# Turning attention probabilities one step later, in 20 steps instead of 19

## The reference: what is computed

```
s = q k^T * scale (+ gate bias, causal or dilated mask)
p = exp(s - max(s)) / sum        # dilated heads: p is weighted by a count of 0 to 3 first
o = p v
x = LayerNorm(alpha * x + concat(o) @ w_out)
```

## Time and profile before

| | us |
|---|---|
| median of three runs | 820.36 |
| profiled execution, its own time | 822.08 |
| its span, first to last instruction | 820.5 |
| PE busy | 797.2 (97%) |
| DVE busy | 634.1 (77%) |
| ACT busy | 508.5 (62%) |
| POOL busy | 78.4 (10%) |

### The profile page before, as it was taken

How to read it: one execution, slowest core, us unless ns; L and a number is a source line. 1 busy time by engine, 2 the same in 40 slices (tenths; PEclk the granted TensorE clock), 3 DMA queues, 4 the chain that set the end, 5 groups by cost and what they waited for, 6 DMA issues and landing times.

```text
span 820.5 us, 12140 instructions
## 1 busy us (share of the span) xinstructions
PE 797.2 (97%) x4364; PEld 688.0 (84%) x4364; DVE 634.1 (77%) x1110; ACT 508.5 (62%) x804; POOL 78.4 (10%) x150
## 2 busy tenths in 40 slices
PE   7899999999999999999999999999999999999995
PEld 7899897789877888888899989877998788888884
DVE  5657868785658999999765586786846699999995
ACT  4755554554546788888555555554454567888873
POOL 3148200020000000000011350000200000000000
PEclk9999999999999999999999999999999999999998
DMA  8954443475334799999755644336643439999951
GB/s 289 344 182 155 144 135 130 139 228 157 105 126 134 246 368 367 364 370 374 259 150 146 209 142 154 105 129 204 209 129 99 145 120 342 367 369 364 370 209 52
DMA packets 122095, 177.06 MB, mean 216 GB/s; under 512 B 10177, under 2 KB 90577, under 8 KB 122033
## 3 DMA queue, kind: packets, MB, share of 16 engines
q1 hardware_dynamic: 120048, 169.56, 62.0%
q0 software_dynamic: 1984, 6.70, 2.9%
HBM read 175.18 MB, written 1.05 MB: 215 GB/s over the span
## 4 chain that ended last, share of the span: by engine, by line
PE 81%; DVE 10%; ACT 4%; issue 2%; DMA 2%; SPq 0%; POOL 0%; DVEq 0%; ACTq 0%; POOLq 0%
PE bank L1557 22%; PE bank L1559 22%; PE bank L1558 22%; DVE w_split L509 3%; DMA raw<-in_w_in_dram 2%; PE bank L1660 2%; PE bank L1724 2%; PE bank L1765 2%; PE bank L1870 2%; DVE xg_lo L1496 1%; ACT w_split L504 1%; PE bank L1756 1%; PE bank L1735 1%; PE bank L1713 1%; PE bank L1785 1%
## 5 line engine op out<-in xcount | busy, mean ns | idle before, releaser
L509 DVE TENSOR_TENSOR w_split<-raw,w_split 128x1024 fp32r<-128x1024 f32 (+3 forms) x336 | 386.0, 1173 | 69.8 <-ACT w_split L504 63.6
L504 ACT ACTIVATE w_split<-raw 128x1024 fp32r<-128x1024 f32 (+3 forms) x336 | 335.4, 1010 | 103.7 <-PE bank L1559 86.2
L1557 PE MATMUL bank<-w_split,xg_hi 128*128 128x512 f32 x256 | 102.9, 402 | 0.0
L1559 PE MATMUL bank<-w_split,xg_lo 128*128 128x512 f32 x256 | 100.1, 391 | 0.0
L1558 PE MATMUL bank<-w_split,xg_hi 128*128 128x512 f32 x256 | 99.9, 390 | 0.0
L1557 PE MATMUL bank<-w_split,xT_hi 128*128 128x384 f32 (+2 forms) x224 | 77.9, 348 | 3.1 <-DVE w_split L509 2.3
L1559 PE MATMUL bank<-w_split,xT_lo 128*128 128x384 f32 (+2 forms) x224 | 76.5, 341 | 0.0
L1558 PE MATMUL bank<-w_split,xT_hi 128*128 128x384 f32 (+2 forms) x224 | 76.2, 340 | 0.0
L1559 PEld LDWEIGHTS bank<-w_split,xg_lo 128*128 128x128 f32 x256 | 48.0, 188 | 10.3
L1557 PEld LDWEIGHTS bank<-w_split,xg_hi 128*128 128x128 f32 x256 | 48.1, 188 | 9.5 <-DVE xg_lo L1496 0.6
L1558 PEld LDWEIGHTS bank<-w_split,xg_hi 128*128 128x128 f32 x256 | 48.2, 188 | 9.0
(11 more groups left out here) (314 smaller groups left out, 1550.9 us busy)
## 6 DMA issues: line engine op xcount, KB each, us to landing
raw<-in_expert_w_gate_dram SPq DMA_DIRECT2D x128, 256.0 KB, 5.8
raw<-in_expert_w_up_dram SPq DMA_DIRECT2D x128, 256.0 KB, 7.8
raw<-in_expert_w_down_dram SPq DMA_DIRECT2D x64, 512.0 KB, 7.8
raw<-in_xattn_w_kv_dram SPq DMA_DIRECT2D x32, 512.0 KB, 4.1
raw<-in_w_in_dram SPq DMA_DIRECT2D x40, 384.0 KB, 4.0
raw<-in_w_mix_out_dram SPq DMA_DIRECT2D x16, 512.0 KB, 3.8
raw<-in_xattn_w_q_dram SPq DMA_DIRECT2D x16, 512.0 KB, 3.4
raw<-in_xattn_w_o_dram SPq DMA_DIRECT2D x16, 512.0 KB, 5.5
```

The lines of the kernel that those rows point to most:

```text
L504: nc.scalar.activation(w_hi[:, i % SPL, 0:w], raw[:, i % RAW, 0:w], ACT.Copy).then_inc(hi_ready, 1)
L509: nc.vector.tensor_tensor(w_lo[:, i % SPL, 0:w], raw[:, i % RAW, 0:w], w_hi[:, i % SPL, 0:w].bitcast(F32), ALU.subtract).then_inc(lo_ready, 1)
L1557: nc.tensor.matmul(o, lhs[0], rhs[0], start=first, stop=False, skip_group_check=shared)
L1559: return nc.tensor.matmul(o, lhs[1], rhs[0], start=False, stop=last, skip_group_check=shared)
```

## The change

Head h is now normalised in step h + 2, turned in step h + 3 and multiplied with the values in step h + 4. The loop has 20 steps. The 29 units are dealt out anew: one unit in each of steps 13 to 19. Probabilities of three heads are kept in one buffer `probs` that also holds the two transposed ones; the guard on their reuse counts turns of three heads before. The exponentials of dilated heads no longer write a sum (it was not used: `softmax_norm` sums the counted ones). DVE's order in a step becomes splits, copies, normalisation, `evac_pT`, maxima, low part of the values.

```diff
+TURNED, VALUED = 3, 4
-        slots = [3, 2, 2] + [2, 1] * 4 + [1, 2] * 2 + [1] * 4
+        slots = [[3, 2, 2] + [2, 1] * 4 + [1, 2] + [1] * 7] * L
...
+        def probs_of(h):
+            if h < HEADS:
+                return probs[:, (h % 3) * 3 * P:(h % 3 + 1) * 3 * P]
+            return probs[:, (h % 2) * 4 * P:(h % 2 + 1) * 4 * P]
...
+        def free_turns(h):
+            return h - 2 if h < HEADS else max(h - 1, HEADS)
...
             def exps(l, h):
-                if h >= 2:
-                    act.wait_ge(pt_done.sem, pt_done.at(l, h - 1))
+                if h >= 3:
+                    act.wait_ge(pt_done.sem, pt_done.at(l, free_turns(h)))
...
-                    acc = sm1 if MLA_H + FOX_H <= h < HEADS else sm
+                    total = {} if MLA_H + FOX_H <= h < HEADS else {"accum_out": sm[:, h, t:t + 1]}
...
@@ ScalarE's loop
-                for s in range(HEADS + 3):
+                for s in range(HEADS + VALUED):
...
-                    if s >= 3 and (s - 3) % 2 == 1:
-                        evac_o(l, s - 3)
+                    if s >= VALUED and (s - VALUED) % 2 == 1:
+                        evac_o(l, s - VALUED)
...
@@ VectorE's loop, behind the splits and copies of the step
+                    if 2 <= s < HEADS + 2:
+                        softmax_norm(l, s - 2)
+                    if TURNED <= s < HEADS + TURNED:
+                        evac_pT(l, s - TURNED)
                     for h in scored(s):
                         softmax_max(l, h)
-                    if in_pair(s - 1) and s % 2 == 0:
-                        softmax_norm(l, s - 1)
-                    if 2 <= s <= HEADS + 1:
-                        evac_pT(l, s - 2)
-                    if 1 <= s <= HEADS and not (in_pair(s - 1) and s % 2 == 0):
-                        softmax_norm(l, s - 1)
...
@@ TensorE's loop, behind the units of the step
-                    if s >= 3 and (s - 3) % 2 == 1:
-                        head_values(l, s - 3)
-                    if 2 <= s <= HEADS + 1:
-                        head_turn(l, s - 2)
+                    if s >= VALUED and (s - VALUED) % 2 == 1:
+                        head_values(l, s - VALUED)
+                    if TURNED <= s < HEADS + TURNED:
+                        head_turn(l, s - TURNED)
```

More of the change, by code:

```diff
@@ L408, in build @@
             fill = list(between(l, ("FQ", 2), ("WO1", 0)))
-            assert sum(slots) == len(fill)
+            assert sum(slots[l]) == len(fill)
             k = 0
             turns.append([])
-            for n in slots:
+            for n in slots[l]:
                 turns[l].append(fill[k:k + n])
                 k += n
-            assert len(turns[l]) == HEADS + 3
+            assert len(turns[l]) == HEADS + VALUED
             ahead_of.append(turns[l][1:] + [[index[l, "WO1", 0], index[l, "WO0", 3]]])
@@ L424, in qk_slot, with turned_of @@
             return (h // 2 + 1) % 2 if in_pair(h) else h % 2
+        def probs_of(h):
+            if h < HEADS:
+                return probs[:, (h % 3) * 3 * P:(h % 3 + 1) * 3 * P]
+            return probs[:, (h % 2) * 4 * P:(h % 2 + 1) * 4 * P]
+        def turned_of(h):
+            if h < HEADS:
+                return probs[:, (9 + h % 2 * 3) * P:(12 + h % 2 * 3) * P]
+            return probs[:, (8 + h % 2 * 4) * P:(12 + h % 2 * 4) * P]
+        def free_turns(h):
+            return h - 2 if h < HEADS else max(h - 1, HEADS)
         def score_bank(h):
@@ L1055, in softmax_max @@
                 if h < HEADS:
-                    if h >= 2:
-                        dve.wait_ge(pt_done.sem, pt_done.at(l, h - 1))
+                    if h >= 3:
+                        dve.wait_ge(pt_done.sem, pt_done.at(l, free_turns(h)))
                     dve.nop().then_inc(paused_v, 1)
@@ L1414, in _ @@
                         copy_job(l, "MV0", lambda t: vx[:, t, 0:512], lambda b: b[:, :])
+                    if 2 <= s < HEADS + 2:
+                        softmax_norm(l, s - 2)
+                    if TURNED <= s < HEADS + TURNED:
+                        evac_pT(l, s - TURNED)
                     for h in scored(s):
                         softmax_max(l, h)
-                    if in_pair(s - 1) and s % 2 == 0:
-                        softmax_norm(l, s - 1)
-                    if 2 <= s <= HEADS + 1:
-                        evac_pT(l, s - 2)
-                    if 1 <= s <= HEADS and not (in_pair(s - 1) and s % 2 == 0):
-                        softmax_norm(l, s - 1)
-                    if s >= 3 and (s - 3) % 2 == 1:
-                        if l == 0 and s == 4:
+                    if s >= VALUED and (s - VALUED) % 2 == 1:
+                        if l == 0 and s == VALUED + 1:
                             dve.wait_ge(const_pool, 57)
-                        evac_o(l, s - 3)
+                        evac_o(l, s - VALUED)
                 for i in range(index[l, "WO1", 1], index[l, "XQ0", 0]):
@@ L1756, in head_values @@
                             ins = nc.tensor.matmul(B_O[k * HD:(k + 1) * HD, q0:T], v[:, t, g - 1 + k, :],
-                                                   pT[:, k, t * T:t * P + T], start=t == 0, stop=t == 1)
+                                                   turned_of(h - 1 + k)[:, t * T:t * P + T], start=t == 0, stop=t == 1)
                     ins.then_inc(o_done.sem, 2)
@@ L1765, in head_values @@
                             ins = nc.tensor.matmul(value_bank(h)[:, dblk * T:(dblk + 1) * T], vx[:, c_, f * P:(f + 1) * P],
-                                                   pT[:, h % 2, c_ * T:(c_ + 1) * T], start=c_ == 0, stop=c_ == 1)
+                                                   turned_of(h)[:, c_ * T:(c_ + 1) * T], start=c_ == 0, stop=c_ == 1)
                     ins.then_inc(o_done.sem, 1)
```

21 lines of the change are left out of this document (10 added, 11 removed).

## The result

The changed kernel takes 835.73 us (median of 4 runs, 834.02 to 836.49), beside 821.32 us for the kernel before (818.98 to 825.62): a ratio of 1.0167, interval 1.012 to 1.0213. The forecast was 827.4 us with a range of 820.5 to 832.5. It had the sign, and half of the size: +7.0 us was expected and +14.4 came, and the time lies 3.2 us above the range. The profiled execution took 836.49 us, 14.4 more than the one before, and 834.8 of them are the span; its mean granted clock is 0.99 as before.

A forecast was written before the change was run, and what follows sets the result against it. TensorE, 97% busy, was taken as bound by a 5.5 us chain from scores to split weights. Per layer 2.7 + 1.2 + 0.2 - 0.6 = 3.5, +7.0 for two, on 820.36 gave 827.4 us, range 820.5 to 832.5.

The forecast's parts named there:

- The chain of the pairs: Dilated pairs: scores through exponentials to usable split weights, 5.43 us, outlasts TensorE's work in steps 14 and 16; +2.7 us per layer.
- The waits for probabilities: Heads' loop: TensorE's waits for normalised probabilities, and small weight waits beside them, go; 0.6 us per layer gained.
- The single heads' cover: Single heads' even steps lose values as work covering the wait for split weights; +1.2 us per layer, bounds 0.4 and 2.4.
- VectorE's order: Normalisation and `evac_pT` ahead of the maxima cost nothing, except in the pairs: 0.2 us per layer, bounds 0 and 1.3.
- the ring: Not forecast: single heads' loop of VectorE's low part, normalisation, copy, maxima and ScalarE's exponentials, split; one turn 7.47 us.
- The clock rival: New TensorE waits in the pairs drop its clock to 1.2 GHz, 1.7 us each; 830.8 or 834.2 us; chance 0.20.

The follow-up runs named there:

- e9: Changed kernel with VectorE's maxima ahead of normalisation and transposes' copy, and GpSimd's rotation done for one dilated head of six: 827.13 us, ratio 1.0062 to before.
- e1: Changed kernel with VectorE doing the maxima first in a step, then normalisation and the copy of the transposes: 829.35 us, ratio 1.0093 to before.
- e8: Changed kernel with GpSimd's rotation of the dilated heads' q and k done for one head of six only: 829.72 us, ratio 1.0108 to before.
- e2: Changed kernel with the weight splits of ScalarE and VectorE one unit further ahead of TensorE: 832.88 us, ratio 1.0137 to before.
- e5: Changed kernel with VectorE's order copy of the transposes, maxima, normalisation last: 829.79 us, ratio 1.0099 to before.
- e7: Changed kernel with the unit moved from step 14 to step 19 given back to step 14: 837.78 us, ratio 1.0201 to before.
- e4: Kernel before the change, with the weight splits one unit further ahead: 818.62 us, ratio 0.9957 to before.
- e6: Changed kernel with copy of the transposes first, then maxima, normalisation last, and splits one unit further ahead: 822.13 us, ratio 1.0006 to before.

## Why the prediction was right in sign and half in size

- **The chain of the pairs** held: 1.83 and 2.27 us for 1.8 and 2.2, through the exponentials, the copy of the values, and both splits. Less 1.35 before, the term is 2.75 us per layer (2.7 forecast).
- **The waits for probabilities** went, together with the small ones beside them: 1.35 and 1.1 us per layer by starts, 0.6 forecast. The error is in the kernel's favour. All waits of the loop before came to 2.7 and 2.4 us by starts, 5.1 in all, where the text had about 4.5.
- **The single heads' cover** was right as a term: with the order put right and the contention short, e9 leaves 0.9 us per layer, and e1 1.95 and 0.9, for 1.2.
- **VectorE's order is the step that failed.** The text had: "They work on heads that are long ready and end before the scores do, so they cost nothing, except in the pairs". That the heads are long ready is true; that the two operations end before the scores do is not. In the step shown above they ran until 82.70, and the scores had ended by 76.96. The normalisation's input is ready, but the engine is not: it comes to the normalisation only behind the split, the split waits for ScalarE's, and that stands behind the last exponentials. So the ring sets when the normalisation starts, and the maxima start behind it. For the single heads the order was priced at nothing (the 0.2 us per layer, 1.3 at most, was for the pairs); it cost them 4.2 us in each layer (after against e1, by starts). I looked at what the two operations wait for, and not at when VectorE's program comes to them. The rows to ask were in the trace of before: the low part of the earlier trace rows is followed by a second one, and that by the maxima without idle time. They start 0.38 us behind their scores (101.36), as they do in e1 when VectorE waits for them, so the engine came just in time, and what is put in between holds them up:

```profile
99.36 2.36 DVE L509 TENSOR_TENSOR w_split<-raw,w_split 128x1024 fp32r<-128x1024 f32 x2 [0.20 <-ACT w_split L504]
101.74 0.29 DVE L1063 CUSTOM_DVE_ANT_0 p_sb<-bank,causal 128x128 f32<-128x128 f32 x1
```

- **The duration.** The text has no duration for a normalisation in the single heads' steps. In a quiet stretch it is 0.55 us (87.03); beside GpSimd it was 1.89, and the negative of the maximum 0.81 for 0.17. The time goes with GpSimd's passes: the two passes of the normalisation end at 81.2 and 82.2, just behind the ends of GpSimd's at 81.10 and 82.08. The Trainium skill ("SBUF — State Buffer", section "Who interferes with whom") says that VectorE's `tensor_scalar` in its faster mode and GpSimd exclude each other for a whole instruction; the trace agrees for these two operations, without showing their mode, and the copy out of PSUM beside them kept its 0.55 us. Not every small operation was stretched: in the kernel before, the negative at 69.73 us kept its 0.17 beside a GpSimd pass from 69.29 to 70.37.
- **The clock rival** did not come in after: its profiled loops have no stretch under 1.00, and its four runs had 0.988 to 0.990. But the reason given, that 2.2 us is below "the only wait here that brought one", misread the trace of before. There the clock also fell behind a wait of 1.41 us, ahead of the transposes of x for the router; the engine did matmuls of 16 to 128 columns from 247.25 to 251.00 in between (us, PE busy, granted clock, DMA share, GB/s):

```profile
247.25 1.32 PE L2064 MATMUL bank<-ident,xs 128*128 128x128 f32 x8 [1.41 <-DVE xs L1161]
```
```profile
251.43:254.84 3.41, 3.41 (x10) 0.50 0.93 251
```

And a drop came behind waits of after's size in a variant. e8 has after's two waits, 1.59 and 2.12 us by modelled ends (2.11 in layer 1); in layer 0 this stretch began 1.3 us behind the second, which ended at 144.03, and in layer 1 there was none:

```profile
145.36:148.77 3.41, 3.41 (x12) 0.50 0.35 129
```

The loops of e1, e2, e5, e7 and e9 have such stretches too. So it was in part luck that the forecast without drops fits after; what decides it is open.

Sum by starts: 2.75 + 6.2 - 1.35 + 0.1 = 7.7 us in layer 0 and 2.75 + 5.2 - 1.1 + 0.1 = 6.95 in layer 1, some 14.6 in all, for 14.4 measured. (The 0.1 is a wait at the loop's end.)

## What to carry to other kernels

When an operation is moved up on an in-order engine, ask not whether its inputs are ready but when the engine gets there, and follow the engine's program once around: if it comes back to itself through another engine, everything between is paid in full, and at its slowest duration, not at its usual one. Work that nobody waits for belongs behind the instruction that another engine is waiting for. Splitting further ahead helps where one link is late (e4), and mostly moves the wait where the ring is too long (e2); with the order put right it helps again (829.79 us in e5, 822.13 in e6).

## What the runs showed of the hardware that was not expected

- VectorE's small scalar operations took up to five times as long beside GpSimd's passes of about 1.0 us: 0.81 us for 0.17 on 2 columns, 1.89 for 0.55 on a normalisation. The weight splits did so in some places only. In e1 two of 768 columns, begun at 74.49 ahead of the rotation, took 1.81 us, as in after (1.83), and the GpSimd pass that came at 75.43 grew to 1.74. One that came while a pass ran, from 68.24, took 1.75, where a quiet one takes 0.95:

```profile
68.32 1.75 DVE L525 TENSOR_TENSOR w_split<-raw,w_split 128x768 fp32r<-128x768 f32 x1 [0.99 <-ACT w_split L520]
```

- TensorE waits 1.41 us ahead of the transposes of x for the router, in every kernel alike (layer 0: at 247 us before, 254 after, 248 in e1). In the profiles of before and after a stretch of 3.41 us at 1.2 GHz follows, in that of e1 one of 10.24. Why the length differs stays open. Half of the 6.8 us between them, 3.4, is what it costs; the executions of e1 spread over 6.6 us (826.27 to 832.86).
